# One-pass maxima in the mLSTM memory, the merging's last branches moved into the output projection, and a gated weight cast in the norms

## The reference

```python
def rmsnorm(x, g):
    y = x * lax.rsqrt(jnp.mean(x * x, axis=-1, keepdims=True) + EPS)
    return y * g
# every layer: h = rmsnorm(x, gain) * (1 + scale) + shift, then a projection of h
# layer 1, mLSTM memory, 8 heads, two directions: each step weighs earlier ones with
    m_t = jnp.maximum(log_inter, jnp.max(logw, axis=-1))
    s = jnp.einsum('bhtd,bhsd->bhts', qc, kc) * jnp.exp(logw - m_t[..., None])
    h = num / jnp.maximum(jnp.abs(den), jnp.exp(-m_t))[..., None]
# layer 2, three branches merged under gates, then projected
    gates = jax.nn.sigmoid(gt + b_gate[l]).reshape(b, s, N_BRANCH, D_MODEL)
    merged = (gates[:, :, 0] * (y_a @ wb[:A_WIDTH])
              + gates[:, :, 1] * (y_b @ wb[A_WIDTH:A_WIDTH + B_WIDTH])
              + gates[:, :, 2] * (y_c @ wb[A_WIDTH + B_WIDTH:]))
    x = x + merged @ w_out[l]
```

## Time and profile before

| | |
|---|---|
| median of 3 runs | 2827.46 us (2826.91 to 2828.77) |
| profiled execution: its own time | 2830.2 us |
| its span | 2828.3 us |
| mean granted TensorE clock | 0.97 of full speed |
| TensorE matmuls busy | 94% of the span |
| VectorE, ScalarE, GpSimd busy | 54%, 32%, 10% |
| mean DMA rate | 83 GB/s |

### The profile page before, as it was taken

How to read it: one execution, slowest core, us unless ns; L and a number is a source line. 1 busy time by engine, 2 the same in 40 slices (tenths; PEclk the granted TensorE clock), 3 DMA queues, 4 the chain that set the end, 5 groups by cost and what they waited for, 6 DMA issues and landing times. The chain is left out here.

```text
span 2828.3 us, 31699 instructions
## 1 busy us (share of the span) xinstructions
PE 2656.9 (94%) x13054; PEld 2146.2 (76%) x13054; DVE 1515.0 (54%) x2043; ACT 914.5 (32%) x1222; POOL 289.0 (10%) x162
## 2 busy tenths in 40 slices
PE   6996999999999999999988999999989899999998
PEld 4874666688888888878766788887676677788887
DVE  6226899874338536461266543444689833433332
ACT  4332434423211212342265332332333622232221
POOL 1111223000000000000000000000240644000000
PEclk9998899999999999999999999999999999999999
DMA  6011101331215424122000223223120232222221
GB/s 267 26 44 50 40 30 45 147 129 68 71 64 183 160 77 169 45 98 81 17 1 31 77 89 111 103 72 107 63 82 16 75 105 82 81 96 91 104 81 61
DMA packets 37035, 236.07 MB, mean 83 GB/s; under 512 B 4128, under 2 KB 5152, under 8 KB 13216
## 3 DMA queue, kind: packets, MB, share of 16 engines
q1 hardware_dynamic: 36896, 234.11, 23.1%
HBM read 231.99 MB, written 2.10 MB: 83 GB/s over the span
## 5 line engine op out<-in xcount | busy, mean ns | idle before, releaser
L368 PE MATMUL pair<-h_high,w_high 128*128 128x512 f32 x2000 | 725.5, 371 | 20.0 <-ACT w_high L300 8.6
L369 PE MATMUL pair<-h_low,w_high 128*128 128x512 f32 x2000 | 720.8, 369 | 0.0
L322 DVE TENSOR_TENSOR w_low<-ring,w_high 128x2048 fp32r<-128x2048 f32 (+5 forms) x164 | 342.3, 2093 | 201.0 <-ACT w_high L300 193.7
L374 PE MATMUL pair<-h_high,w_low 128*128 128x512 f32 x2000 | 448.3, 366 | 0.0
L368 PEld LDWEIGHTS pair<-h_high,w_high 128*128 128x128 f32 x2000 | 379.9, 190 | 88.7 <-issue 17.3
L369 PEld LDWEIGHTS pair<-h_low,w_high 128*128 128x128 f32 x2000 | 380.3, 190 | 65.7 <-issue 1.4
L374 PEld LDWEIGHTS pair<-h_high,w_low 128*128 128x128 f32 x2000 | 349.1, 189 | 62.8
L300 ACT ACTIVATE w_high<-ring 128x2048 fp32r<-128x2048 f32 (+4 forms) x167 | 289.9, 1737 | 311.7 <-PE pair L374 204.3
L368 PE MATMUL pair<-high,w_high 128*128 128x512 f32 (+1 forms) x704 | 249.1, 363 | 1.0 <-DVE low L1263 1.0
L369 PE MATMUL pair<-low,w_high 128*128 128x512 f32 (+1 forms) x704 | 249.0, 363 | 0.0
L1257 DVE TENSOR_TENSOR gate<-gate,pair 128x512 f32<-128x512 f32 (+1 forms) x66 | 51.3, 777 | 238.3 <-PE pair L374 220.9
(11 more groups left out here) (459 smaller groups left out, 3908.1 us busy)
## 6 DMA issues: line engine op xcount, KB each, us to landing
ring<-in_w_up SPq DMA_DIRECT2D x66, 1024.0 KB, 4.8
ring<-in_w_ada SPq DMA_DIRECT2D x32, 1024.0 KB, 4.9
ring<-in_w_down SPq DMA_DIRECT2D x32, 704.0 KB, 4.0
ring<-in_w_ada0r SPq DMA_DIRECT2D x16, 1024.0 KB, 4.8
ring<-in_w_merge_b SPq DMA_DIRECT2D x14, 1024.0 KB, 4.8
ring<-in_w_down SPq DMA_DIRECT2D x8, 1024.0 KB, 5.0
ring<-in_w_att_in SPq DMA_DIRECT2D x6, 1024.0 KB, 4.8
ring<-in_w_heads SPq DMA_DIRECT2D x6, 1024.0 KB, 5.0
```

Of the source, the lines that this page charges most:

```text
L322: (on or self.nc.vector).tensor_tensor(self.w_low[:, n % 2, 0:floats], self.ring[:, chunk % RING, 0:floats], self.w_high[:, n % 2, 0:float ...
L368: self.nc.tensor.matmul(out[:, a:e], w_high[:, k, at], high[:, k, a:e], start=k == 0, stop=False)
L369: self.nc.tensor.matmul(out[:, a:e], w_high[:, k, at], low[:, k, a:e], start=False, stop=False)
L374: mm = self.nc.tensor.matmul(out[:, a:e], w_low[:, k, at], high[:, k, a:e], start=False, stop=k == kt - 1)
```

## The change

It has three parts. **Memory:** `top` becomes fp32r and holds the rounded maxima in rows 0 to 63 and the rest (maxima less rounded maxima) in rows 64 to 127; the weights are a column of a new tile `both`, in which the 64x64 identity stands twice, made by GpSimd. A matmul is then fp32r and adds both parts. **Merging:** the last two branches, q = 22 and 23, are multiplied and added by VectorE in the projection's stage (`LastBranches`); GpSimd makes the low parts of three tiles (`LOWS`) instead of six, and VectorE those of tiles 3 to 7 in the projection. TensorE there goes tile by tile over both blocks of the first chunk (`first_blocks`). **Norms:** GpSimd's cast waits for VectorE's last coefficient (`coef_ready`).

```diff
@@ Norm.pool
+        pool.wait_ge(K.coef_ready.sem, K.coef_ready.base + 1)
         K.split_half(K.nc.gpsimd, self.first + 1, 0).then_inc(K.half_ready.sem, 1)
@@ Norm.dve
-                chain.step(nc.vector.scalar_tensor_tensor(
+                op = nc.vector.scalar_tensor_tensor(
                     K.coef[:, j, :], K.mod[:, self.scale * KD:self.scale * KD + KD, j], 1.0, self.gain,
-                    ALU.add, ALU.mult))
+                    ALU.add, ALU.mult)
+            if j < len(self.parts) - 1:
+                chain.step(op)
+        op.then_inc(K.coef_ready.sem, 1)
...
                     chain.sync()
+                    dve.wait_ge(K.coef_ready.sem, K.coef_ready.base + 1)
@@ residual_split_stage
+    halved = order is not None and K.fresh is not None
...
-                    if n == 0:
+                    if halved and n == 0:
                         pe.wait_ge(K.half_ready.sem, K.half_ready.base + 1)
-                    elif n == kt // 2:
+                    elif n == (kt // 2 if halved else 0):
                         pe.wait_ge(K.high_ready.sem, K.split_number[first] + 1)
-                    pe.wait_ge(low_ready.sem, low_ready.base + n + 1)
+                    if n >= split:
+                        pe.wait_ge(low_ready.sem, low_ready.base + n - split + 1)
...
-                for n, k in enumerate(order):
+                for n, k in list(enumerate(order))[highs:]:
                     if last is not None:
                         last.act(act, n)
                     nc.scalar.activation(high[:, k, :], raw(k), ACT.Copy).then_inc(high_ready.sem, 1)
...
-            for n, k in enumerate(order or range(split, kt if raw is not None else 0)):
+            tiles = range(kt if raw is not None else 0) if order is None else order
+            for n, k in list(enumerate(tiles))[split:]:
                 if last is not None:
                     last.dve(dve, chain, n)
-                dve.wait_ge(high_ready.sem, high_ready.base + n + 1)
+                if n >= highs:
+                    dve.wait_ge(high_ready.sem, high_ready.base + n - highs + 1)
@@ gate_conv_stage, VectorE
             chain.step(nc.vector.tensor_copy(top[0:R, :], high[:, 0:LAT]))
+            chain.sync()
+            chain.step(nc.vector.tensor_tensor(top[R:2 * R, :], high[:, 0:LAT], top[0:R, :].bitcast(F32), ALU.subtract))
@@ mlstm_stage
+        both = stack.enter_context(K.temp("both", [P, 64], F32R))
...
-            nc.gpsimd.memset(top[64:128, :], 0.0)
             chain = Chain(pool, K.pool_chain)
+            for half in range(2):
+                r = slice(64 * half, 64 * half + 64)
+                chain.step(nc.gpsimd.tensor_copy(both[r, :], K.ident[r, r]))
+            chain.sync()
...
-                    mm = nc.tensor.matmul(tops(d, 0, LAT), K.ident[:, row:row + 1].broadcast_to([P, P]), top[:],
+                    mm = nc.tensor.matmul(tops(d, 0, LAT), both[:, row:row + 1].broadcast_to([P, P]), top[:],
@@ merge_stage
-            for f in range(EARLY):
+            for f in range(LOWS):
                 pool.wait_ge(next_high.sem, next_high.base + f + 1)
...
-                for c in range(3):
+                for c in range(3 if f < KD - 1 else 1):
@@ new
+class LastBranches:
+    def act(self, act, n):
+        if n == KD - 1:
+            act.wait_ge(self.merged.sem, self.merged.base + 1)
+    def dve(self, dve, chain, n):
+        nc, out, part = self.K.nc, self.out, self.part
+        if n in (4, 5):
+            chain.sync()
+            chain.step(nc.vector.tensor_tensor(part, self.gates[n - 4], self.banks[n - 4], ALU.mult))
+            chain.sync()
+            op = nc.vector.tensor_tensor(out, out, part, ALU.add)
+            if n == 4:
+                chain.step(op)
+            else:
+                op.then_inc(self.merged.sem, 1)
@@ mix2
             residual_split_stage(K, "w2_out", K.h_high, K.h_low, KD, 2, LAT, None, raw=lambda k: cc[:, k, :],
-                                 ahead=False, split=6)
+                                 ahead=False, split=3, highs=6, order=list(range(KD)), last=LastBranches(K, hd, cc))
```

More of the change, by code:

```diff
@@ L192, in __init__ @@
         self.ctx_copied = sem("ctx_copied")
+        self.coef_ready = sem("coef_ready")
         self.norm_scaled = sem("norm_scaled")
@@ L711, in dve @@
             if self.scale is None:
-                chain.step(nc.vector.tensor_copy(K.coef[:, j, :], self.gain))
+                op = nc.vector.tensor_copy(K.coef[:, j, :], self.gain)
             else:
-                chain.step(nc.vector.scalar_tensor_tensor(
+                op = nc.vector.scalar_tensor_tensor(
                     K.coef[:, j, :], K.mod[:, self.scale * KD:self.scale * KD + KD, j], 1.0, self.gain,
-                    ALU.add, ALU.mult))
+                    ALU.add, ALU.mult)
+            if j < len(self.parts) - 1:
+                chain.step(op)
+        op.then_inc(K.coef_ready.sem, 1)
         for m in range(len(self.steps) + 1):
@@ L752, in end @@
         self.K.pool_half.base += 1
+        self.K.coef_ready.base += 1
         for c in (self.K.ctx_inverted, self.K.ctx_spread, self.K.ctx_copied):
@@ L1296, in residual_split_stage @@
 def residual_split_stage(K, name, high, low, kt, per, tokens, gate, raw=None, ahead=True, stats=True,
-                         reload=False, beside=None, split=0, order=None, last=None):
+                         reload=False, beside=None, split=0, highs=0, order=None, last=None):
     nc = K.nc
@@ L1412, in _ @@
                 squares.act_end(act)
-        if order is not None:
+        if halved:
             @block.gpsimd
@@ L1484, in residual_split_stage @@
     if raw is not None:
-        high_ready.base += kt - split
+        high_ready.base += kt - highs
         low_ready.base += kt - split
@@ L3370, in mix1 @@
         sb = lambda name, shape: outer.enter_context(K.temp(name, shape))
-        keysT, floorT, top = sb("keysT", [P, 6, 64]), sb("floorT", [P, 4, 64]), sb("top", [P, LAT])
+        keysT, floorT = sb("keysT", [P, 6, 64]), sb("floorT", [P, 4, 64])
+        top = outer.enter_context(K.temp("top", [P, LAT], F32R))
         qT, kT, sig = sb("qT", [P, 4, LAT]), sb("kT", [P, 4, ALL]), sb("sig", [P, 8, LAT])
@@ L3606, in merge_stage @@
     chunk_of = {n + half: m for m, n in gates_of.items() for half in range(2)}
-    LAST, EARLY = 4 * PAIRS - 1, 6
+    LAST, EARLY, LOWS = 4 * PAIRS - 1, 6, 3
     halves = lambda ap: ap.rearrange("p (a b) -> p a b", a=2)
@@ L3889, in merge_stage, with __init__, pe, end @@
     for c, n in ((gates_done, 24), (lru_done, 4), (branch_done, 24), (gated, 24), (high_ready, KD), (rates_in, 4),
-                 (curves, 4), (rooted, 4), (soft_ready, 1), (gelu_in, 4), (conved, 4), (low_ready, KD), (used, 24),
-                 (radic, 4), (rate_ready, 1), (scaled, 4), (y_ready, 4), (inner, 4), (gelu, 4), (merged, KD),
+                 (curves, 4), (rooted, 4), (soft_ready, 1), (gelu_in, 4), (conved, 4), (low_ready, KD), (used, 22),
+                 (radic, 4), (rate_ready, 1), (scaled, 4), (y_ready, 4), (inner, 4), (gelu, 4), (merged, KD - 1),
                  (next_high, EARLY)):
         c.base += n
+class LastBranches:
+    def __init__(self, K, hd, cc):
+        self.K, self.out, self.part = K, cc[:, KD - 1, :], hd[:, 10, :]
+        self.gates = [hd[:, (q + 4) % 10, :] for q in (22, 23)]
+        self.banks = [K.psum[:, 2048:2560], K.psum[:, 2560:3072]]
+        self.merged = K.last_scaled
+    def pe(self, pe, n):
+        pass
+    def act(self, act, n):
[12 more added lines that the diff above has]
+                op.then_inc(self.merged.sem, 1)
+    def end(self):
+        self.merged.base += 1
 def mix2(K):
```

## The result

The changed kernel takes 2809.89 us at the median of 4 runs (2806.07 to 2812.39), beside 2827.97 (2826.91 to 2828.77) for the kernel before: a ratio of 0.9935, with an interval of 0.9918 to 0.9952. That is 18.1 us faster; forecast were 2808.1 us and, from the sum, 19.4. In four further sets the kernel before stood at 2827.98 to 2828.57. The changed kernel spreads by 6 us from run to run, the one before by 2 in this set and by 2 to 9 in the others, so a difference of less than about 2 us between two builds says little by itself. In what follows "the whole" is the changed kernel with all its parts.

The account below looks back on a forecast made before the run. TensorE's work and its few standstills were taken to bound the kernel. Memory 10.8, merging 5.5 and norms 3.1 sum to 19.4 us, making the median 2808.1 us; bounds of the parts 2804 to 2813, range 2802 to 2815.

Parts of the forecast that it names:

- The loop's 7.5: Memory, heads 2 to 7: each shorter spread saves 1.25 us, all on the path, 6 x 1.25 = 7.5 us.
- The start was to save 1.5 and 1.6: Memory stage's start: spreads of heads 0 and 1, taken at 0.7 us each, save 1.5 and 1.6 us.
- GpSimd's start was to gain 0.2: Memory's start: zeroing of 0.52 us goes, two 64x64 casts of 0.15 each come; 0.2 us gained.
- the 0.94 at 1312.31: Merging: gap between stages where TensorE itself is last, model for a 0.9 us gap before the projection, 3.4 us earlier.
- The clock's 2.5: Projection's first block: the half-clock excess of 2.54 us goes if the clock stays up over the short gap.
- The wait of 0.4 at tile 5: Projection: TensorE reaches tile 5 before VectorE's low part is ready and waits 0.4 us.
- the two cases of the race: Front norm: VectorE's first y or GpSimd's cast issues first; gain 1.3 us or 0.5 us, 0.8 taken.
- Rival 1: Projection: clock low despite the short gap, the 2.54 us stay and the 0.4 wait goes; 2810.2 us, chance 0.14.
- rival 2: Memory: another chain (ScalarE's exponentials, VectorE's products) takes over, half the loop's 7.5 us lost; 2811.9 us, chance 0.11.
- rival 4: Memory: spread isn't a single pass despite its type, only GpSimd's 0.2 us remains; 2818.7 us, chance 0.05.
- Rival 5: Memory: TensorE's clock falls as work shrinks and gaps stay; three such heads give 2853 us, slower; chance 0.04.
- Rival 3: Norms: casts come too late or hold low parts longer, the part is nothing; 2811.2 us, chance 0.10.

Follow-up runs that it names:

- projection_held: The whole, but TensorE waits before the projection's first matmul until the merging's last product is scaled; 2818.72 us.
- norms_only: The kernel before plus only the wait of GpSimd's cast for VectorE's coefficients; 2828.57 us, ratio 1.0002.
- whole_again: The changed kernel with all its parts, unaltered, run again beside the single-part kernels; 2809.55 us, ratio 0.9937.
- filled_without_norms: The whole plus four idle TensorE matmuls before each of six norm openings, without the wait of GpSimd's cast for the coefficients; 2803.64 us, ratio 0.9914.
- openings_filled: The whole plus four idle TensorE matmuls, results never read, before the first matmul of each of six norm openings; 2799.96 us, ratio 0.9896.

## Why the prediction was right, and where it was not

**Memory, 10.8 forecast.** Right in its mechanism and, within its spread, in size: 11.3 by the run, 10.0 in the stage by the trace. The loop's 7.5 came as 6 x 1.26, since the wait of 1.50 moves with the work ahead of it, as put. Two terms were too high. The start was to save 1.5 and 1.6 and saved 2.56, just under its bound of 2.7: the first spread saved 1.64, but the second took 1.55 and not 0.7, with the clock at 0.50 from 5 to 10 us behind the first spread, where it had been 0.83. And GpSimd's start was to gain 0.2 and lost 0.13: the two casts of 64x64 take 0.52 for both, 0.26 each, not 0.15. VectorE's subtraction (0.69) is hidden: the idle time ahead of block 7 is 3.28 instead of 3.90.

**Merging, 5.5 forecast.** 6.4 by the trace, 6.6 by the run. The start is 3.96 us earlier where 3.4 stood, because TensorE crosses the end of the stage in a gap of 0.32 and not 0.9: the 0.94 at 1312.31 was the wrong neighbour. Why the same crossing takes 0.94 there stays open. The clock's 2.5 came as put (2.45, from 13.74 to 11.29 us for the first two blocks). The wait of 0.4 at tile 5 didn't come: VectorE's instructions follow each other at 0.60 to 0.72 us, its waits on itself included, so it begins its three last low parts at 2386.09, 3.9 us behind its start, and ends the first of them after some 4.5 where 5.0 stood; TensorE reaches tile 5 at 2386.97, 4.7 us behind its own, and the low part is there. Both measures lie above the upper bound of 6.2, which had no room for a gap under 0.7. `projection_held` shows the two big terms come and go together.

**Norms, 3.1 forecast: the step that failed.** The sum said 2.3 at four openings and 0.8 at the front. What each opening's first matmul gained was 0.51, 0.81, 0.23 and 0.49 where 0.6, 0.9, 0.3 and 0.5 stood, and 0.66 at the front, between the two cases of the race. So 2.7 of 3.1 arrived at the place where I had put it. What failed is the step from there to the end: it isn't seen in the time. The three comparisons of whole kernels give -0.4, 1.6 and 3.7 us, where the openings alone give 3.0. My own guess on the way, that an earlier start is half lost because the clock's rise doesn't move with it, fell too: the rest of the openings sums to 123.1 with the wait and 123.2 without. What takes it in the trace of `norms_only` is, as far as it can be followed, the clock in stages that nobody edited. Whether that belongs to the build or is drawn anew in each execution stays open in part. The whole and `whole_again` are the same program, and their traces differ in such an episode: in the memory's last head, behind the same pause of 2.63 us, the sums take 7.75 us in the first and 6.10 in the second.

```profile
1509.26 7.91 PE L3117 MATMUL pair<-val,prob 128*128 128x129 f32 x54 [2.63 <-ACT xT L3175]
```

```profile
1511.54 6.27 PE L3117 MATMUL pair<-val,prob 128*128 128x129 f32 x54 [2.63 <-ACT xT L3175]
```

The clock is 0.57 in the 4 us from 1510 of the first and 1.00 in the 4 us from 1512 of the second. So an episode of 1.6 us can come and go with the same program. But all eleven runs of `norms_only` lie between 2827.16 and 2829.26, and a loss drawn anew each time would hardly take as much from each of them. Why this build loses it isn't shown.

**The sum and the rivals.** 18.1 by the medians against 19.4: the norms gave less by 1.5 to 3.5, the memory less by 0.8 by its trace, the merging more by 0.9. That the total comes out within 1.3 us owes something to luck, since a part of 3.1 can't be seen in it. The profiled pair shows 22.8, of which 1.5 is the first weight's arrival (TensorE starts at 8.05 us instead of 9.58; of the other traces most have 8.1 to 8.2, `filled_without_norms` 9.72, so it isn't the work of an edit). The memory's 10.0, the merging's 6.4 and the openings' 2.5 leave some 2.4 us to stages that no edit touches. The range's lower end was added up wrongly: the bounds of the parts, 14.1 to 22.2 us, give 2805 to 2813 and not 2804.

Rival 1 (clock low in the projection) is excluded by the windows at 1.00, rival 2 (another chain in the memory) by the unchanged 1.50, rival 4 by the two records of each spread. Rival 5 as put, three heads at half clock, is excluded by windows at 1.00 from 1392 to 1509. A small form of it stays open: the episode in the last head, behind a pause of 2.6 us that stood there before, is in four of the ten traces with the short spread and in none of the four with the long one, which is too few to tell from chance. Rival 3, the norms part nothing (2811.2), came true in part; the measured 2809.89 lies between it and the forecast.

## What to carry to other kernels

Where two engines end a stage late by the same amount, cost and test the edits together: each half alone gave 2.2 and 0.8 us and both gave 6.4. Of a removed wait read both the gap and the clock behind it, and where a pause of about 2 us can't be removed, a few idle matmuls in it may be worth more than making it shorter, if they end before the pause does. An edit worth less than 2 us is judged by the distances inside its own stage, over several kernels with and without it, since unedited stages move by 1.5 us from build to build, and by as much between two executions of one program.

## What the runs showed of the hardware

- Four idle matmuls (1.13 us at the high clock) had the clock at 1.00 from the first real matmul on in three openings whose first matmuls ran at the low clock in the whole, and saved 6.6 us there. At layer 0's FFN they didn't: the idle matmuls themselves take 1.63 us, in part at the low clock, and the first four real ones 2.07 where the heads show 1.20.

```profile
613.06 1.63 PE L389 MATMUL pair<-ident 128*128 128x128 f32 x8 [0.30 <-PEq L1328]
615.26 2.07 PE L400 MATMUL pair<-h_high,w_high 128*128 128x512 f32 x4 [0.57 <-ACT h_high L703]
```

- A gap of 0.32 us left the clock at 1.00; gaps of 3.03, 3.15 and 4.32 at the same place took it down. In between, the gap's length doesn't decide alone: in the kernel before the clock was 0.50 shortly after a gap of 1.74 us at 821.89 and 1.00 behind the same gap at 1031.15 (in the 4 us from 1031), and behind the 2.63 us in the memory's last head it was low in four of fourteen traces.
- Beside GpSimd's cast VectorE's copy of 128x8 took 1.04 us, and 0.17 alone; the first y of the front was held for 0.8 us more than its usual 0.74 where GpSimd issued 0.06 us ahead.
- `openings_filled`, at 2799.96 us, is faster than the kernel before and the whole, at 0.9896 of the first.
